# One layer of a hybrid decoder: six of eight pairs of gate projections as seven block products, taken ahead of the branch outputs

## The chip, the cores and the metric

The kernel runs on one core of a Trainium2 chip, as one launch. The metric is the device time of the launch in microseconds (us); lower is better. TensorE is PE in the profile (PEld its weight loads), VectorE DVE, ScalarE ACT, GpSimd POOL; SP issues most transfers.

## The reference, cut to what matters

For 512 prompt rows and 32 sample rows (544 columns once transposed) one layer is computed. The stretch that matters:

```
h = rmsnorm(x, norm1_g) * (1 + sc1) + sh1                  # 544 x 1024
u_in, gate_c, gate_b, q, k, v, g_conv, g_attn = split_projection(h @ w_in)
y_conv = (gate_b * short_conv(gate_c * u_in)) @ w_conv_out  # 1024 -> 1024
y_attn = attn_o @ w_attn_out                                #  512 -> 1024
mixed  = (sigmoid(g_conv) * y_conv + sigmoid(g_attn) * y_attn) @ w_o
x = x + gt1 * mixed          # then a second norm and 16 routed experts
```

## The kernel before

Tokens are columns, split in halves t = 0, 1 of 272 (`HALF`). All projections run as *pieces*, numbered m: one piece makes 128 output channels from 8 chunks (`KC`) of 128 input channels. For accuracy each operand is split into a rounded part and a remainder (`whi`, `wlo`; `hHi`, `hLo`), and `project` multiplies hi with hi, lo with hi and hi with lo: 24 matmuls of 128x128 by 128x272 for a half, 48 for a piece. The result stands in PSUM bank t until some engine has read it (`bank_free[t]`).

Order of the pieces: 0 to 35 q, k, v; 36 to 59 the convolution's inputs; then the branch stage from `C0` = 60 to 91, a loop over f = 0..7 with four pieces each: j = 0 conv output (source `ybHi`/`ybLo`), j = 1 its gate, j = 2 attention output (`oHi`/`oLo`, only 4 chunks, 24 matmuls), j = 3 its gate; then `D0` = 92 to 99 the output projection from `mixHi`/`mixLo`. Half pieces are counted by G = 2m + t. Attention for the prompt and the sample runs between half pieces; its last slots (`decode`, 28 to 31), eight transposes of convolution states and the splitting of `yb` and `oT` stand between piece 59 and the branch stage.

A piece's weights pass through a ring of four (`RING`): SP loads `wraw[m % 4]` once the remainder of piece m - 4 is made; ACT writes `whi` when PE has left that slot (`split_hi`), DVE writes `wlo` (`split_lo`), both for piece m + 3 while PE is at m (`LEAD`). In front of each load of the branch stage's loop SP issues one copy of 1 MB of a key or value cache from DRAM to DRAM (`shift_v3`).

In the branch stage ACT copies every output half out of PSUM (`gyc`) or takes its sigmoid (`gsg`), and DVE multiplies, adds and splits the mix. In the output projection DVE scales each half into `op` (L2218), which is what frees its bank; PE transposes it (`mixed_T`), and `residual` adds it to the rows `x2` of the input. The first `residual` waits for all three loads of `x2` (`xr_in`, 48) and stands in DVE's queue between the two halves of piece 93. SP loads `x2` behind piece 95's weights, after a wait for piece 90 (L825); the modulation rows (`tokt`, `toks`) wait for the last mix (L830); the 32 sample rows come last (L838).

Every engine runs its own queue in the order written; `own` lets DVE wait for its own instruction.

## Time and profile before

| | us |
|---|---|
| time, median of 3 runs (range) | 1102.28 (1101.98 to 1103.21) |
| the profiled execution: span from first to last instruction | 1098.3 |
| outside the span, against the median | 4.0 |
| PE busy in the span | 1069.9 |
| DVE, ACT, POOL busy | 535.5, 355.4, 183.0 |
| branch stage, first matmul to the output projection's first | 572.04 to 740.91 |

The span is that of one profiled execution; the times are of runs without a profile. A view by windows gives the busy time of each engine in a stretch; a timeline lists instructions in order of time, with the idle time ahead of them and what ended it in brackets.

### The profile page before, as it was taken

To read this page: it belongs to the slowest core of one execution; us is meant where nothing else is said; L and a number is where in the kernel's file an instruction comes from. 1 tells how busy PE (TensorE), PEld (TensorE's weight loads), DVE (VectorE), ACT (ScalarE), POOL (GpSimd) and SP (SyncE) were. 2 spreads that over 40 slices of the span, in tenths; PEclk is the share of its full clock that TensorE was granted. 3 is DMA by queue.
4 is the path that set the end of the run, shared out by engine and by line. 5 is a ranking of instruction groups with operands and counts; after the bars stand their busy time and mean duration, and the time that the engine had idled before them with its cause. 6 is when DMAs were issued, how large, how long until landed. Compare 5 with 4: busy or idle time off the path is not lost. (4 is left out here: it accounts for less than half of the span.)

```text
span 1098.3 us, 29565 instructions
## 1 busy us (share of the span) xinstructions
PE 1069.9 (97%) x12413; PEld 929.2 (85%) x12413; DVE 535.5 (49%) x1226; ACT 355.4 (32%) x670; POOL 183.0 (17%) x262
## 2 busy tenths in 40 slices
PE   4899999999999999999999999999999999999997
PEld 3799999999999998898779999999956677777753
DVE  1845565555556545444354444445586333233326
ACT  5623333332433322232244444443332111101112
POOL 1344343343330200000000000000001211121121
PEclk9999999999999999999999999999999999999999
DMA  9969989989888566655999887639679999999996
GB/s 346 341 201 330 387 298 356 387 284 376 310 289 307 175 234 208 235 192 197 410 341 329 281 316 274 205 128 317 240 312 383 368 420 421 421 424 424 422 391 246
DMA packets 161946, 343.95 MB, mean 313 GB/s; under 512 B 11691, under 2 KB 116571, under 8 KB 147310
## 3 DMA queue, kind: packets, MB, share of 16 engines
q1 hardware_dynamic: 149086, 318.64, 78.6%
q0 software_dynamic: 5936, 16.05, 4.1%
q10 hardware_dynamic: 6832, 7.93, 2.1%
q8 instruction: 70, 1.15, 0.4%
q14 instruction: 22, 0.18, 0.0%
HBM read 321.82 MB, written 108.85 MB: 392 GB/s over the span
## 5 line engine op out<-in xcount | busy, mean ns | idle before, releaser
L1035 PE MATMUL psum<-hHi,whi 128*128 128x272 f32 x1200 | 354.1, 295 | 0.3 <-ACT rb L1672 0.3
L1035 PE MATMUL psum<-hLo,whi 128*128 128x272 f32 x1200 | 346.4, 289 | 0.0
L1035 PE MATMUL psum<-hHi,wlo 128*128 128x272 f32 x1200 | 345.9, 288 | 0.0
L1035 PEld LDWEIGHTS psum<-hHi,whi 128*128 128x128 f32 x1200 | 226.2, 189 | 9.1 <-issue 7.5
L1035 PEld LDWEIGHTS psum<-hHi,wlo 128*128 128x128 f32 x1200 | 226.4, 189 | 0.0
L1035 PEld LDWEIGHTS psum<-hLo,whi 128*128 128x128 f32 x1200 | 226.0, 188 | 0.0
L1846 DVE TENSOR_TENSOR wlo<-wraw,whi 128x1024 fp32r<-128x1024 f32 x100 | 133.7, 1338 | 74.9 <-ACT whi L1566 74.8
L1395 PE MATMUL psum<-e,xs 128*32 128x256 f32 x3072 | 169.1, 379 | 0.9 <-DVE xs L2470 0.8
L1395 PEld LDWEIGHTS psum<-e,xs 128*32 128x32 f32 x3072 | 116.3, 110 | 50.6 <-issue 2.5
L2696 POOL DMA_INDIRECT xg<-x_tok,piece x45 | 43.1, 958 | 432.7 <-DMA x_tok<-h 246.9
L1566 ACT ACTIVATE whi<-wraw 128x1024 fp32r<-128x1024 f32 x100 | 104.9, 1051 | 23.7 <-PE psum L1035 23.6
L1408 PE MATMUL psum<-e,hT 128*32 128x256 f32 x1440 | 80.8, 379 | 1.1 <-DMA e<-in_w_dram 0.6
L1775 ACT ACTIVATE sil<-psum 128x128 f32<-128x128 f32 x48 | 13.1, 277 | 198.1 <-PE psum L1395 198.0
L1408 PEld LDWEIGHTS psum<-e,hT 128*32 128x32 f32 x1440 | 55.8, 110 | 23.6 <-DMA e<-in_w_dram 1.7
L2476 DVE TENSOR_TENSOR hid<-sil,psum 128x128 f32<-128x128 f32 x48 | 13.7, 285 | 117.0 <-ACT sil L1775 116.8
L2632 POOL TENSOR_TENSOR t<-rb,ropec 128x272 f32<-128x272 f32 x48 | 38.9, 810 | 165.9 <-ACT rb L1672 145.9
L1672 ACT ACTIVATE rb<-psum 128x272 f32<-128x272 f32 x48 | 18.9, 395 | 104.9 <-PE psum L1035 104.9
L2012 DVE COPY kTs<-psum 128x1024 f32<-128x1024 f32 x18 | 22.1, 1225 | 47.6 <-PE psum L1127 47.6
L2634 POOL TENSOR_TENSOR shb<-shb,ropes 128x272 f32<-128x272 f32 x48 | 40.4, 841 | 1.5 <-DVE shb L2126 1.5
L1035 PE MATMUL psum<-mixHi,whi 128*128 128x272 f32 x128 | 37.5, 293 | 0.0
L1035 PE MATMUL psum<-ybHi,whi 128*128 128x272 f32 x128 | 37.1, 290 | 0.0
L1035 PE MATMUL psum<-mixLo,whi 128*128 128x272 f32 x128 | 37.1, 290 | 0.0
(399 smaller groups left out, 1535.4 us busy)
## 6 DMA issues: line engine op xcount, KB each, us to landing
e<-in_w_dram SPq DMA_DIRECT2D x96, 1024.0 KB, 14.2
wraw<-in_w_in_dram SPq DMA_DIRECT2D x76, 512.0 KB, 6.5
out_dram<-in_cache_k_dram SPq DMA_DIRECT2D x32, 1022.0 KB, 9.7
out_dram<-in_cache_v_dram SPq DMA_DIRECT2D x32, 1022.0 KB, 7.8
adar<-in_w_ada_dram SPq DMA_DIRECT2D x36, 512.0 KB, 7.7
kvr<-in_cache_k_dram SPq DMA_DIRECT2D x8, 2048.0 KB, 7.8
kvr<-in_cache_v_dram SPq DMA_DIRECT2D x8, 2048.0 KB, 11.2
out_dram<-in_cache_k_dram SPq DMA_DIRECT2D x8, 1016.0 KB, 9.7
```

The source lines that it names most:

```text
L1035: mm = pe.matmul(psum[:, t, 0:HALF], w[:, slot, k, :], x[:, k, cols], start=(k == 0 and n == 0), stop=(k == k_n - 1 and n == 2))
L1395: mm = pe.matmul(psum[32 * n:32 * n + 32, g, 0:2 * P].rearrange("p (w f) -> p w f", w=2), xs[:, q, k, 32 * g:32 * g + 32], (e13[q] if w13 ...
L1408: mm = pe.matmul((psum[:, 3 + g, 0:DQ] if u else first_y(g))[32 * n:32 * n + 32], hT[:, fc, 32 * g:32 * g + 32], w2_[:, fc, DQ * n:DQ * n ...
L1566: act.activation(whi[:, slot], wraw[:, slot], ACT.Copy).then_inc(hi_done, 1)
L1672: act.activation(dst, psum[:, t, 0:HALF], ACT.Copy).then_inc(bank_free[t], 1)
L1775: act.activation(sil[:, g, :], psum[:, g, 0:P], ACT.Silu).then_inc(sil_done, 1)
L1846: dve.tensor_tensor(wlo[:, slot], wraw[:, slot], whi[:, slot].bitcast(F32), ALU.subtract)\
L2012: dve.tensor_copy(kTs[:, 8 * P:16 * P], turned[:, 8 * P:16 * P]).then_inc(ktr_dve, 1)
L2476: dve.tensor_tensor(hid[:, g, :], sil[:, g, :], psum[:, g, P:2 * P], ALU.mult).then_inc(hid_done, 1)
L2632: pool.tensor_tensor(t1[:, t, :], rb[:, t, :], ropec[:, cols], ALU.mult).then_inc(rot_done, 1)
L2634: pool.tensor_tensor(shb[:, t, :], shb[:, t, :], ropes[:, cols], ALU.mult)\
L2696: pool.indirect_dma_start(xg[:, q, g, :], None, x_pieces, bass.IndirectOffsetOnAxis(piece[:, q, g:g + 1], 0)).then_inc(xg_in[q], 16)
```

## The change

The gate projections come first: pieces 60 to 75 are the 8 pairs (conv gate, attention gate), then 8 attention outputs (from `O0` = 76), then 8 conv outputs (from `Y0` = 84). Pairs 0 and 1 are ordinary pieces. The other six (`PAIRS`) are made by Strassen's method in Winograd's form: weights of a pair as 2 x 2 blocks (output piece by input half), `h` as 2 x 2 blocks (input half by token half), seven products of 4 chunks each, 12 matmuls for a product (4 chunks by three passes). The four sums of weight blocks are made by POOL for each pair, the four sums of `h` blocks once, three by DVE in `column_sums` and one by POOL. ACT and DVE split every operand (`operand_hi`, `operand_lo`, `columns_hi`, `columns_lo`); products rotate through four PSUM banks and DVE adds them up (`added`), ACT keeping two. Sigmoids are taken in place in SBUF for the six pairs. DVE multiplies the outputs with the gates straight from PSUM. The decode slots 28 to 31 and the state transposes now stand between half pieces 120 to 123. The whole stage is written out instead of looped. The cache copies keep their place, one ahead of each load from piece 64 on. Regions for the gates now lie where `x2` will be, and `x2`'s load waits for the last mix (`g_lo`, 16).

Not shown below: the placement of the buffers, `half_lo` (the remainder of a 4-chunk piece), `columns_hi` and `columns_lo` (split of a column sum), `operand_hi` (ACT's copy, waits for `pool_sum` or the load, and for the product of the pair before that used the slot), the use of one semaphore for several (`logits_pe`, `moved_act`, `rows_pe`).

```diff
+G_P = 2 * KC
+O0 = C0 + G_P
+Y0 = O0 + KC
+PAIR_F0 = 2
+PAIRS = KC - PAIR_F0
+PAIR0 = C0 + 2 * PAIR_F0
+QUART = KC // 2
+ORDER = ("A11", "A12", "S2", "S1", "S3", "S4", "A22")
+AT = {name: i for i, name in enumerate(ORDER)}
+KEPT = {"A11": 1, "S1": 2}
+ADDED = {"A12": 1, "S2": 2, "S3": 4, "S4": 6, "A22": 7}
...
+                if C0 + RING <= m < D0:
+                    shift_v3(m - C0 - RING)
+                last = m - RING
+                if PAIR0 <= last < O0:
+                    n = (last - PAIR0) // 2
+                    sp.wait_ge(w_lo, 7 * n + 7)
+                    sp.wait_ge(pool_sum, 4 * n + 5)
+                else:
+                    sp.wait_ge(lo_done, nth(last) + 1)
+                sp.dma_start(piece_place(m), piece_source(m)).then_inc(raw_in[m % RING], 16)
+                if m < C0 + RING:
+                    cache_units(m)
                 if m == D0 + RING - 1:
 
-                    sp.wait_ge(grp, 2 * (D0 - 1))
+                    sp.wait_ge(g_lo, 2 * KC)
                     for a in (0, 2):
                         sp.dma_start(x2[:, a:a + 2, :], xall_v[:, a:a + 2, :]).then_inc(xr_in, 16)
...
-            pe.wait_ge(yo_lo, KC)
-            with pe.Fori(0, KC) as f:
-                for j in range(RING):
-                    pe.wait_ge(lo_done, 4 * f + (C0 + j + 1))
-                    if j == 2:
-                        pe.wait_ge(yo_lo, KC + 1)
-                    xhi, xlo = ((ybHi, ybLo), (hHi, hLo), (oHi, oLo), (hHi, hLo))[j]
-                    for t in range(2):
-                        project(None, j, xhi, xlo, t, k_n=AC if j == 2 else KC, free=4 * f + (C0 + j))
+            h_halves = [[(hHi[:, QUART * r:QUART * r + QUART, HALF * c:HALF * c + HALF],
+                          hLo[:, QUART * r:QUART * r + QUART, HALF * c:HALF * c + HALF]) for c in range(2)] for r in range(2)]
+            moving = {"A11": h_halves[0][0], "A12": h_halves[1][0], "S2": (hTHi[1], hTLo[1]), "S1": (hTHi[0], hTLo[0]),
+                      "S3": (hTHi[2], hTLo[2]), "S4": h_halves[1][1], "A22": (hTHi[3], hTLo[3])}
...
+            def paired(n):
+
+                for i, name in enumerate(ORDER):
+                    r = 7 * n + i
+                    pe.wait_ge(w_lo, r + 1)
+                    if n == 0 and name in built:
+                        pe.wait_ge(t_lo, built[name])
+                    if r >= 4:
+                        product_read(r - 4)
...
+                    xhi, xlo = moving[name]
+                    for k in range(QUART):
+                        for j, (w, x) in enumerate(((whalf, xhi), (wlow, xhi), (whalf, xlo))):
+                            mm = pe.matmul(psum[:, r % 4, 0:HALF], w[:, i, k, :], x[:, k, :],
+                                           start=(k == 0 and j == 0), stop=(k == QUART - 1 and j == 2))
+                    mm.then_inc(w_pe, 1)
+
+            for n in range(PAIRS):
+                paired(n)
+            for m in range(O0, D0):
+                pe.wait_ge(lo_done, nth(m) + 1)
+                if m == O0:
+                    pe.wait_ge(yo_lo, 1)
+                elif m == Y0:
+                    pe.wait_ge(yo_lo, KC + 1)
+                for t in range(2):
...
+                    if m < Y0:
+                        project(m, m % RING, oHi, oLo, t, k_n=AC, free=nth(m))
+                    else:
+                        project(m, m % RING, ybHi, ybLo, t, free=nth(m))
...
+            def gates_sigmoid(n, part):
+
+                act.wait_ge(p_dve, 7 * n + 6 + part)
+                out = gates[PAIR_F0 + n][:, part, :]
+                act.activation(out, out, ACT.Sigmoid).then_inc(gate_done, 1)
+
...
+            for n in range(PAIRS):
+                if n == 0:
+                    columns_hi(2, 1, pool_sum)
+                operand_hi(n, "S3")
+                operand_hi(n, "S4")
+                kept(n, "A11", p1, 2)
+                operand_hi(n, "A22")
+                if n == 0:
+                    columns_hi(3, 3, t_sum)
+                else:
+                    gates_sigmoid(n - 1, 0)
+                following(n, 0)
+                following(n, 1)
+                kept(n, "S1", p5, 5)
+                if n:
+                    gates_sigmoid(n - 1, 1)
+                if n == 1:
+                    act.wait_ge(so_ev, 4)
+                    act.wait_ge(yb_done, 2 * KC)
+                    act.activation(oHi[:, :, :], oT[:, :, :], ACT.Copy).then_inc(yo_hi, 1)
+                following(n, 2)
+                following(n, 3)
...
+            for m in range(O0, D0 + 1):
+                if m >= O0 + 1:
+                    split_hi_at(m + LEAD)
+                if m < O0 + QUART:
+                    if m == O0:
+                        act.wait_ge(w_pe, 7 * PAIRS)
+                        act.wait_ge(yb_done, 2 * KC)
+                    for k in range(2 * (m - O0), 2 * (m - O0) + 2):
+                        act.activation(ybHi[:, k, :], yb[:, k, :], ACT.Copy).then_inc(yo_hi, 1)
...
+            def operand_lo(n, name):
+
...
+                dve.tensor_tensor(wlow[:, i], src, whalf[:, i].bitcast(F32), ALU.subtract).then_inc(w_lo, 1)
...
+            def column_sums():
+
+                dve.wait_ge(spv_pe, K_UNITS)
+                dve.wait_ge(new_out, 16 * GROUPS * (AC + 1))
...
+                own(dve.tensor_tensor(t1_[:, :, :], b12h, b11h, ALU.subtract))
+                own(dve.tensor_tensor(hTtmp[1][:, :, :], b12l, b11l, ALU.subtract))
+                own(dve.tensor_tensor(t1_[:, :, :], t1_[:, :, :], hTtmp[1][:, :, :], ALU.add))
+                dve.sem_inc(t_sum, 1)
+                own(dve.tensor_tensor(t2_[:, :, :], b22h, t1_[:, :, :], ALU.subtract))
+                own(dve.tensor_tensor(t2_[:, :, :], t2_[:, :, :], b22l, ALU.add))
+                dve.sem_inc(t_sum, 1)
+                dve.wait_ge(so_pe, 2)
+                own(dve.tensor_tensor(t4_[:, :, :], b21h, t2_[:, :, :], ALU.subtract))
+                own(dve.tensor_tensor(t4_[:, :, :], t4_[:, :, :], b21l, ALU.add))
+                dve.sem_inc(t_sum, 1)
...
+                if G == slot_of["O", 1] + DEC_G0:
+                    column_sums()
+                if G == 2 * PAIR0 - 4:
+                    operand_lo(0, "A11")
+                    operand_lo(0, "A12")
+                if G == 2 * PAIR0 - 2:
+                    columns_lo(1, 2)
+                    columns_lo(0, 2)
+
+            def added(n, name, out, other):
+
+                r = 7 * n + AT[name]
+                dve.wait_ge(w_pe, r + 1)
+                dve.wait_ge(p_dve, 7 * n + ADDED[name] - 1)
+                dve.tensor_tensor(out, psum[:, r % 4, 0:HALF], other, ALU.add).then_inc(p_dve, 1)
+
...
+            for n in range(PAIRS):
+                if n:
+                    added(n - 1, "A22", gate_part(n - 1, 1, 0), u3[:, :])
+                operand_lo(n, "S2")
+                operand_lo(n, "S1")
+                if n == 0:
+                    columns_lo(2, 3)
+                operand_lo(n, "S3")
+                dve.wait_ge(p_act, 2 * n + 1)
+                added(n, "A12", gate_part(n, 0, 0), p1[:, :])
+                operand_lo(n, "S4")
+                added(n, "S2", u2[:, :], p1[:, :])
+                operand_lo(n, "A22")
+                if n == 0:
+                    columns_lo(3, 4)
+                dve.wait_ge(p_act, 2 * n + 2)
+                dve.wait_ge(p_dve, 7 * n + 2)
+                dve.tensor_tensor(u25[:, :], u2[:, :], p5[:, :], ALU.add).then_inc(p_dve, 1)
+                if n + 1 < PAIRS:
+                    operand_lo(n + 1, "A11")
+                added(n, "S3", u3[:, :], u2[:, :])
+                dve.wait_ge(p_dve, 7 * n + 4)
+                dve.tensor_tensor(gate_part(n, 1, 1), u3[:, :], p5[:, :], ALU.add).then_inc(p_dve, 1)
+                added(n, "S4", gate_part(n, 0, 1), u25[:, :])
+                if n + 1 < PAIRS:
+                    operand_lo(n + 1, "A12")
+                if n == 1:
+                    dve.wait_ge(yo_hi, 1)
+                    dve.tensor_tensor(oLo[:, :, :], oT[:, :, :], oHi[:, :, :].bitcast(F32), ALU.subtract).then_inc(yo_lo, 1)
...
+            for i in range(LEAD):
+                half_lo(O0 + i)
+            for m in range(O0, D0):
+                if m + LEAD < Y0:
+                    half_lo(m + LEAD)
+                else:
+                    split_lo((m + LEAD) % RING, nth(m + LEAD) + 1)
+                if m < Y0:
+                    f = m - O0
+                    if m == O0:
+                        dve.wait_ge(gate_done, 2 * PAIRS)
                     for t in range(2):
...
+                        part = gates[f][:, 1, HALF * t:HALF * t + HALF]
+                        dve.wait_ge(grp, 2 * nth(m) + t + 1)
+                        dve.tensor_tensor(part, psum[:, t, 0:HALF], part, ALU.mult).then_inc(bank_free[t], 1)
+                    if f < QUART:
+                        for k in range(2 * f, 2 * f + 2):
+                            dve.wait_ge(yo_hi, k + 2)
+                            dve.tensor_tensor(ybLo[:, k, :], yb[:, k, :], ybHi[:, k, :].bitcast(F32),
+                                              ALU.subtract).then_inc(yo_lo, 1)
+                    continue
+                f = m - Y0
+                for t in range(2):
+                    cols = slice(HALF * t, HALF * t + HALF)
+                    if f == 0 and t == 0:
+                        dve.wait_ge(state_out, 16 * (2 * GROUPS + 2))
+                    elif f >= 1:
+                        dve.wait_ge(g_lo, 2 * f - 1 + t)
+                    dve.wait_ge(grp, 2 * nth(m) + t + 1)
+                    dve.tensor_tensor(gmx[:, t, :], psum[:, t, 0:HALF], gates[f][:, 0, cols], ALU.mult)\
+                       .then_inc(bank_free[t], 1)
+                    dve.wait_ge(bank_free[t], nth(m) + 1)
+                    own(dve.tensor_tensor(gmx[:, t, :], gmx[:, t, :], gates[f][:, 1, cols], ALU.add))
+                    hi = mixHi[:, f, cols]
+                    own(dve.tensor_scalar(hi, gmx[:, t, :], 1.0, None, ALU.mult))
+                    dve.tensor_tensor(mixLo[:, f, cols], gmx[:, t, :], hi.bitcast(F32), ALU.subtract).then_inc(g_lo, 1)
...
+            pool.wait_ge(so_pe, 2)
+            pool.wait_ge(spv_pe, K_UNITS)
+            pool.wait_ge(rows_ev, 3)
+            for n, (out, part) in enumerate(((hTsum[2], hHi), (hTtmp[3], hLo))):
+                pool.tensor_tensor(out[:, :, :], part[:, high, cols[1]].bitcast(F32), part[:, low, cols[1]].bitcast(F32),
+                                   ALU.subtract).then_inc(zrow_done, 1)
+            pool.wait_ge(zrow_done, 4 * AC + 4)
+            pool.tensor_tensor(hTsum[2][:, :, :], hTsum[2][:, :, :], hTtmp[3][:, :, :], ALU.add).then_inc(pool_sum, 1)
+
+            for n in range(PAIRS):
+                m = PAIR0 + 2 * n
+                a, b = wraw[:, m % RING], wraw[:, (m + 1) % RING]
+                s1, s2, s3, s4 = (wsum[:, AT[name]] for name in ("S1", "S2", "S3", "S4"))
+                pool.wait_ge(raw_in[(m + 1) % RING], 16 * ((m + 1) // RING + 1))
+                pool.wait_ge(raw_in[m % RING], 16 * (m // RING + 1))
+                if n:
+                    pool.wait_ge(w_pe, 7 * (n - 1) + AT["S1"] + 1)
+                else:
+                    pool.wait_ge(grp, 2 * (PAIR0 - RING + AT["S1"] // 2 + 1))
+                pool.tensor_tensor(s1, b[:, low, :], b[:, high, :], ALU.add).then_inc(pool_sum, 1)
+                pool.wait_ge(pool_sum, 4 * n + 2)
+                pool.tensor_tensor(s2, s1, a[:, low, :], ALU.subtract).then_inc(pool_sum, 1)
+                if n:
+                    pool.wait_ge(w_pe, 7 * (n - 1) + AT["S4"] + 1)
+                else:
+                    pool.wait_ge(grp, 2 * (PAIR0 - RING + AT["S4"] // 2 + 1))
+                pool.wait_ge(pool_sum, 4 * n + 3)
+                pool.tensor_tensor(s4, a[:, high, :], s2, ALU.subtract).then_inc(pool_sum, 1)
+                pool.tensor_tensor(s3, a[:, low, :], b[:, low, :], ALU.subtract).then_inc(pool_sum, 1)
```

## Rows read from the trace of the kernel before

**Rows 1.** The page: busy time by slice, and granted clock.
```profile
PE   4899999999999999999999999999999999999997
PEclk9999999999999999999999999999999999999999
```

**Rows 2.** Waits of PE: total, times, longest, us.
```profile
PE psum L1035 <- ACT rb L1672: 0.3, 1, 0.3
```

**Rows 3.** Windows: the branch stage; columns PE, PEld, DVE, ACT, POOL, PEclk, DMA share, GB/s.
```profile
572.10:740.90 168.80, 168.80 (x1345) 168.80 (x1345) 73.57 (x111) 78.69 (x112) 1.03 (x2) 1.00 0.75 257
```

**Rows 4.** Timeline of PE ahead of the branch stage: start, duration, instruction, idle before.
```profile
571.13 1.08 PE L1187 MATMUL psum<-ident,ps__110 128*128 128x32 f32 x8 [0.27 <-DVE ps__110 L2037]
```

**Rows 5.** Groups by line and shape: busy us, mean ns of one, idle before.
```profile
L1846 DVE TENSOR_TENSOR wlo<-wraw,whi 128x1024 fp32r<-128x1024 f32 x100 | 133.7, 1338 | 74.9 <-ACT whi L1566 74.8
...
L2172 DVE TENSOR_TENSOR gmx<-gsg,gyc 128x272 f32<-128x272 f32 x16 | 7.1, 443 | 14.7 <-ACT gsg L1698 14.7
...
L2049 DVE TENSOR_TENSOR ybLo<-yb,ybHi 128x544 fp32r<-128x544 f32 x8 | 5.3, 720 | 0.8 <-ACT ybHi L1680 0.7
...
L2159 DVE TENSOR_TENSOR oLo<-oT,oHi 128x2176 fp32r<-128x2176 f32 x1 | 2.4, 2425 | 2.1 <-ACT oHi L1688 2.1
...
L1566 ACT ACTIVATE whi<-wraw 128x1024 fp32r<-128x1024 f32 x100 | 104.9, 1051 | 23.7 <-PE psum L1035 23.6
...
L1698 ACT ACT_TABLE_LOAD x8 | 10.3, 1283 | 0.1
...
L2632 POOL TENSOR_TENSOR t<-rb,ropec 128x272 f32<-128x272 f32 x48 | 38.9, 810 | 165.9 <-ACT rb L1672 145.9 <-issue 17.7 <-POOL QB L2647 2.2
...
L2652 POOL COPY kTn<-kT 128x32 f32<-128x32 f32 x12 | 2.5, 206 | 12.7 <-DVE kT L1961 12.6
```

**Rows 6.** Timeline of DVE around 218 us.
```profile
219.94 0.47 DVE L2126 STREAM_SHUFFLE shb<-rb 128x272 f32<-128x272 f32 x1
220.88 1.73 DVE L1846 TENSOR_TENSOR wlo<-wraw,whi 128x1024 fp32r<-128x1024 f32 x1 [0.47 <-ACT whi L1566]
```

**Rows 7.** Timeline of POOL in the same stretch.
```profile
220.03 0.77 POOL L2632 TENSOR_TENSOR t<-rb,ropec 128x272 f32<-128x272 f32 x1 [0.66 <-POOL QB L2647]
220.75 0.77 POOL L2634 TENSOR_TENSOR shb<-shb,ropes 128x272 f32<-128x272 f32 x1
```

**Rows 8.** Windows of DMA: a branch-stage stretch, the output projection's start, the experts.
```profile
651.00:660.00 9.00, 9.00 (x74) 9.00 (x73) 4.96 (x10) 4.45 (x7) 0.00 (x0) 1.00 0.90 320
...
736.00:755.00 19.00, 19.00 (x154) 18.99 (x153) 8.67 (x18) 3.32 (x5) 0.00 (x0) 1.00 0.98 311
...
900.00:950.00 50.00, 50.00 (x932) 36.58 (x928) 17.91 (x49) 6.91 (x18) 8.68 (x10) 1.00 1.02 421
```

**Rows 9.** Timeline of SP's DMA queue at the start of the output projection.
```profile
735.09 0.81 SPq L827 DMA_DIRECT2D x<-in_x_prompt_dram  x2
...
743.50 0.34 SPq L832 DMA_DIRECT2D tokt<-mod_rows  x1
...
745.28 2.70 SPq L838 DMA_DIRECT2D x<-in_x_sample_dram  x1
```

**Rows 10.** Timeline of DVE in the output projection's second piece.
```profile
754.82 0.09 DVE L2189 MEMSET sqp<- 128x40 f32 x1 [4.13 <-DMA x<-in_x_sample_dram]
...
756.13 0.17 DVE L2221 TENSOR_TENSOR op<-psum,modT 128x32 f32<-128x32 f32 x1
```

**Rows 11.** Timeline of PE at the transposes behind it.
```profile
756.56 0.60 PE L1269 MATMUL psum<-ident,op 128*128 128x128 f32 x4
```

**Rows 12.** Timelines of PE: equal matmul groups at the start, and the last matmuls.
```profile
15.96 3.54 PE L958 MATMUL psum<-adarD,cT 128*32 128x128 f32 x64 [1.79 <-DMA adarD<-in_w_ada_dram]
23.04 1.95 PE L958 MATMUL psum<-adar,cT 128*32 128x128 f32 x64
...
1091.38 0.28 PE L1524 MATMUL psum<-stat,fold 128*128 128x1 f32 x2
```

**Rows 13.** Window at the end; columns as in Rows 3.
```profile
1094.00:1095.00 1.00, 0.00 (x0) 0.00 (x0) 0.81 (x1) 0.00 (x0) 0.00 (x0) 0.73 0.95 366
```

More of the change, by code:

```diff
@@ L238, in _build @@
     toks_at -= toks_at % 32
-    assert masks_at <= toks_at and toks_at + YB_EARLY * NT * 4 <= rope_at
     zrow = Region(top - 2048 - 64)("zrow", [P, D // 2])
-    ybHi = Region(toks_at)("ybHi", [P, KC, NT], F32R)
     ybLo = Region(yb_at)("ybLo", [P, KC, NT], F32R)
+    oLo = Region(oT_at)("oLo", [P, AC, NT], F32R)
+    r = Region(yb_at + KC * NT * 4)
+    ybHi = r("ybHi", [P, KC, NT], F32R)
+    r = Region(masks_at)
+    early_gates = [r(f"sg{f}", [P, 2, NT]) for f in range(2)]
+    assert r.at <= rope_at
+    oHi = r("oHi", [P, AC, NT], F32R)
+    assert r.at <= top - 2048 - 64
     r = Region(c_region)
@@ L860, in _ @@
             load_e2(0, 0)
-            for j in range(RING):
-                shift_v3(slice(KC - 1, KC), j)
-            sp.wait_ge(grp, 2 * N_P)
+            for i in range(RING * (KC - 1), RING * KC):
+                shift_v3(i)
+            sp.wait_ge(grp, 2 * nth(N_P))
             sp.dma_start(iota[:, :], k_small[:, 96:96 + TS]).then_inc(late_in, 16)
@@ L1610, in decode @@
                                    accum_out=sst[:, half, 2:3]).then_inc(ss_exp, 1)
-            for G in range(2 * C0):
+            for G in range(2 * PAIR0):
                 m, t = divmod(G, 2)
@@ L1700, in _ @@
-            split_hi_at(D0 + LEAD)
+                if kind(m) == "g":
+                    f, j = divmod(m - C0, 2)
+                    act.wait_ge(grp, G + 1)
+                    act.activation(gates[f][:, j, HALF * t:HALF * t + HALF], psum[:, t, 0:HALF], ACT.Sigmoid)\
+                       .then_inc(bank_free[t], 1)
+                if G == STATES_G:
+                    act.wait_ge(rows_pe, 2)
+                    for n in range(2):
+                        act.activation(ltok[:, 512 * n:512 * n + 512], psum[0:18, 6 + n, :], ACT.Copy).then_inc(rows_ev, 1)
@@ new lines, in kept, with following @@
+            def kept(n, name, dst, free):
+                r = 7 * n + AT[name]
+                act.wait_ge(w_pe, r + 1)
+                if n:
+                    act.wait_ge(p_dve, 7 * (n - 1) + free)
+                act.activation(dst[:, :], psum[:, r % 4, 0:HALF], ACT.Copy).then_inc(p_act, 1)
+            def following(n, i):
+                if n + 1 < PAIRS:
+                    for name in (("A11",), ("A12",), (), ("S2", "S1"))[i]:
+                        operand_hi(n + 1, name)
+                else:
+                    split_hi_at(O0 + i)
@@ L2054, in _, with columns_lo @@
+            def columns_lo(i, at):
+                dve.wait_ge(t_hi, at)
+                dve.tensor_tensor(hTLo[i][:, :, :], hTsum[i][:, :, :], hTHi[i][:, :, :].bitcast(F32), ALU.subtract)\
+                   .then_inc(t_lo, 1)
+            for G in range(2 * PAIR0):
                 decode(G - DEC_G0)
```

342 lines of the change are left out of this document (184 added, 158 removed).

## The prediction

> **What bounds the kernel now.** I read the page's slices first, then the waits, then windows of the stage, then timelines for prices. The slices say that PE is busy from the second slice to the last but one, at a granted clock of nine tenths or more [rows 1]. In the waits, the line that holds PE back for a product's bank (L1035) has lost 0.3 us once in the whole kernel [rows 2]. The window of the branch stage makes it exact: PE is busy 168.80 of 168.80 us, 1.00 of the clock, while DVE, ACT and the DMA engines stand idle for much of it [rows 3]. So matmuls saved here shorten the kernel, as long as PE finds its operands. From the same row one matmul takes 168.80 / 1345 = 0.1255 us, so a product of 12 matmuls takes 1.51 us, a half piece of 24 takes 3.01 us, and a pair as seven products 10.54 us.
>
> **Matmuls removed.** An ordinary pair is 96 matmuls, a Strassen pair 84. Six pairs save 72 x 0.1255 = 9.0 us. The 0.27 us that PE waits in the transposes ahead of the stage [rows 4] may go too, since other matmuls now stand between them: -9.3 us in all. ACT loses nearly all of its table loads in the stage (the group shown is 8 at 1.28 us [rows 5]) and many copies out of PSUM. I price that at nothing: ACT works 78.69 of 168.80 us there and PE waits for it nowhere [rows 3].
>
> **The price of a sum, and what POOL does to DVE.** The added work is POOL's and DVE's, both with two inputs in SBUF. DVE alone makes 1024 elements in 1.22 us undisturbed; 544 take 0.72 and 272 take 0.44 us, and 2176 take 2.43 [rows 5]. By that line 512 elements cost 0.69 and 1088 cost 1.29 us. ACT's 512 cost about 0.61. An addition out of PSUM of 272 elements I take at the 0.44 of `gmx`. POOL's nearest rows are 272 elements in 810 ns and a copy of 32 in 206 ns [rows 5]: 2.35 ns an element, with one input against two. A weight sum (512) is then some 1.33 us and a column sum (1088) 2.65; if the 0.81 had no fixed part, 1.5 and 3.2.
>
> The page of groups hides what the two do to each other. DVE's `wlo` at 220.88 took 1.73 us [rows 6]. POOL's operation of 0.77 us had begun at 220.75 [rows 7], so it overlapped `wlo` for 0.64 us, and `wlo` lost 1.73 - 1.22 = 0.51 us: DVE nearly stood still. The shuffle at 219.94, with one input, ran beside POOL's operation of 220.03 in its usual 0.47 us. I therefore charge each POOL operation of this stage in full against DVE's two-input operations that stand ready, and nothing against DVE's additions out of PSUM.
>
> The Trainium skill has a rule for this, which speaks against the change: "SBUF — State Buffer", section "SBUF: two separate sides", calls the shared port pair an exclusive lock held for the whole instruction, between GpSimd and a VectorE operation with two SBUF inputs; the trace agrees, with 0.51 us lost of 0.64. Its page "GPSIMD Engine Reference", § 3.1, has 4497 ns for 2048 fp32 elements on GpSimd. With the fixed part above, that is an estimate of 1.27 and 2.48 us for the two sums, and the total would come about 1 us lower.
>
> **The first pair.** PE has five half pieces between the last transposes and pair 0, 5 x 3.01 = 15.06 us, and wants S2 (third in the order) two products later, at 18.1. By then the shared port must have passed: DVE's seven operations of `column_sums` (7 x 1.29 = 9.0), the remainders of A11 and A12 (1.4), two column remainders (2.6), that of S2 (0.7), together 13.7 us; and POOL's three operations on columns and its first three weight sums (3 x 2.65 + 3 x 1.33 = 12.0), on which S2 itself depends. That is 25.7 us and some 0.5 for hand-overs, against 18.1: PE waits 8.1 us. Up to A22, whose column sum is last, another 0.9: **+9.0 us**. The bounds are 0 (the queues run side by side) and 11.5 (POOL at the upper price).
>
> **The later pairs.** In 10.54 us DVE has seven remainders (4.8), two SBUF additions (0.9) and five out of PSUM (2.2), 7.9 us; POOL has 5.3 us. Two-input work and POOL's together are 11.0 against 10.54, and DVE's queue is in order, so the additions that free the four banks stand behind a blocked remainder. I put the lateness at 0.9 a pair for pairs 3 to 6, 2.3 for the second (it inherits the first's), and a further 2.1 where DVE makes `oLo` at once (2.43 us [rows 5]) ahead of the next pair's remainders: with the parts overlapping, **+7.4 us**, bounds 0.4 and 13. At the entry to piece 76, its remainder stands behind A22's addition in DVE's queue, 0.44 + 0.69 and a hand-over: **+1.3 us**.
>
> **Attention outputs.** A piece lasts 3.01 us. DVE has 0.69 + 2 x 0.44 + 2 x 0.72 = 3.0 us in each of the first four, exactly PE's pace. The DMA engines must bring some 1.5 MB in each 3.01 us (0.5 MB of weights and the 1 MB cache copy ahead of them), 500 GB/s; the most that the trace shows is 421 at a share of 1.02, and this stage reached 320 at 0.90 [rows 8]. At 421 the load lags 0.6 us a piece. Of five pieces the ring hides about half: **+1.5 us**, bounds 0.5 and 4. In the conv outputs (6.02 us a piece) both fit.
>
> **The output projection.** This is a moved step. Now SP issues `x2` at 735.09, 5.8 us before the projection starts at 740.91, then the modulation rows at 743.50 and the sample rows at 745.28 [rows 9]. DVE's first `residual` waits 4.13 us for those last rows, to 754.82 [rows 10]. PE takes the transposes behind it at 756.56 without a wait, with the operand finished only at 756.30 [rows 10, 11]: its slack is some 0.2 us. After the change `x2` waits for the last mix, which DVE makes about 2.2 us into the projection (multiplication, addition, rounding, remainder behind the last half), 8.0 us later than now. The bytes are the same, and the DMA engines are full from 736 to 755 [rows 8], so everything lands 8.0 later. Behind the waiting `residual` in DVE's queue stands the second half's `op` (L2218), which frees the bank and feeds the transposes: **+7.8 us**. The lower bound: 311 GB/s over 18.8 us is 5.8 MB, which at 421 takes 13.9, so 2.9 us remain.
>
> **The clock.** At the end of the kernel the last matmul stands at 1091.38 [rows 12] and the granted clock of the window from 1094 has dropped to 0.73 [rows 13], a fall some 2.8 us after the work ended. A pause of 7.8 us lets it fall to 1.2 GHz. At the start, 64 equal matmuls took 3.54 us behind a wait and 1.95 at full clock [rows 12]: **+1.6 us**. The same after the first pair's pause I price at nothing, as DVE is still what PE waits for there; without that cover it costs 1.6 as well.
>
> **Sum.** -9.3 + 9.0 + 7.4 + 1.3 + 1.5 + 7.8 + 1.6 = +19.3 us. The profiled span of 1098.3 becomes 1117.6; the 4.0 us between span and median stay: 1121.6, say **1121 us**.
>
> **The rivals.** The bound below which this kernel cannot be told from no change is about 0.2%, 2.2 us.
>
> *POOL does not hold DVE* (the one that can end on the other side). DVE's row has one clear case of it, and a remainder may be long for another reason. Then the first pair's 9.0 and the later pairs' 7.4 shrink to `oLo`'s share, about 1: 1121 - 15.5 = 1106. It becomes faster once `x2` lands at the lower bound too, -4.9 and -1.6: 1099. It decides if PE waits for remainders less than 4 us in the stage. Chance 0.16, in half of it not slower.
>
> *The rows of x cost little.* The queue at 736 to 755 still carries cache copies that will be gone by then; the first `residual` waits only 2.9 us more than now and the clock stays: -4.9 - 1.6, 1114 to 1115. Chance 0.16.
>
> *The lateness is given back.* The experts' DMA engines are full at 421 GB/s while PE is busy 50 of 50 us there [rows 8]; if their weights set the pace later on, weights that run ahead during the pauses make up for them, and only the early terms stay: near 1102. Against it, PE does not wait there now. Chance 0.07.
>
> *Steeper prices.* POOL at 1.5 and 3.2 us, attention outputs at 4 us: +2.5, +4, +2.5: 1130. Chance 0.13.
>
> *The products aren't made as said*, for instance matmuls at another pitch than 0.1255 us because operands are parts of larger tiles: nothing in the rows speaks for it; it would move the 9.0 by its share. I fold it into the range.
>
> The forecast holds the remaining 0.48. Its own range is 1115 to 1127. The range for 8 in 10 leaves out the far ends of the first and the last rival: 1100 to 1129. Faster: half of the first rival and some of the third, 0.11. Same: 0.08. Slower: 0.81.
>
> **What would show it.** In the new profile 504 matmuls should stand on one line of paired products. PE should have waits on ACT or DVE for S2 of the first pair of 7 to 9 us, remainders of 512 elements whose mean is well above 0.69 us with POOL's sums beside them, and 1.3 us for a POOL weight sum. DVE's first wait for the sample rows should be about 12 us, with PEclk below 9 after it. Remainders of 0.69 us beside POOL's sums would make the largest terms wrong; a DVE wait near 4 us would remove the projection's; and a window of the experts with PE idle would show that what was lost could be given back.

## The result, and the profile after

| | before | after |
|---|---|---|
| median, us (range) | 1102.13 (1101.52 to 1103.21, 4 runs) | 1128.66 (1126.67 to 1130.05, 4 runs) |
| span of the profiled execution | 1098.3 | 1124.6 |
| PE busy in the span | 1069.9 | 1070.7 |
| DVE, ACT, POOL busy | 535.5, 355.4, 183.0 | 596.3, 338.3, 230.5 |

The kernel became slower by a ratio of 1.0239 (95% interval 1.0224 to 1.0253). 1121 was forecast, with a range of 1100 to 1129, so the sign was right and the size was 7.7 us short: the median lies 0.3 us inside the upper end of the range, and above the forecast's own range of 1115 to 1127. The profiled execution is the fastest of the four, 2.0 us under their median.

The page's slices, as in [rows 1]:

```profile
PE   4999999999999999999997997997999999999997
PEclk9999999999999999999998999998999999999999
```

PE now has three thin slices, each of 28 us: number 22 (the first pair), 25 (the attention outputs) and 28 (the output projection). The waits of PE name them (engine, out and line, what was waited for, then us in total, times and longest). Before there was one such line on a product's bank, with 0.3 us [rows 2]:

```profile
PE psum L1318 <- DVE wlow L2223: 11.2, 7, 5.8
...
PE psum L1069 <- DVE sg L2416: 6.4, 5, 2.5
PE psum L1344 <- DVEq L2490: 5.5, 1, 5.5
...
PE psum L1069 <- DVE wlo L2208: 1.1, 1, 1.1
PE psum L1069 <- DVE op L2474: 1.1, 1, 1.1
```

L1318 is the paired products, with their remainders as holder; L1069 with `sg` the attention outputs, where a bank waits for DVE's multiplication; L1344 the transposes of the output projection. The timeline of PE puts the waits in order of time (start, duration, instruction, idle before):

```profile
602.84 0.59 PE L1318 MATMUL psum<-hHi,whalf 128*128 128x272 f32 x1 [5.75 <-DVE wlow L2223]
...
618.36 0.39 PE L1318 MATMUL psum<-hHi,whalf 128*128 128x272 f32 x1 [1.35 <-DVE wlow L2223]
629.84 0.39 PE L1318 MATMUL psum<-hHi,whalf 128*128 128x272 f32 x1 [0.64 <-DVE wlow L2223]
633.12 0.39 PE L1318 MATMUL psum<-hTHi,whalf 128*128 128x272 f32 x1 [1.52 <-DVE wlow L2223]
...
676.50 0.40 PE L1069 MATMUL psum<-oHi,whi 128*128 128x272 f32 x1 [1.13 <-DVE wlo L2208]
...
700.73 0.36 PE L1069 MATMUL psum<-oHi,whi 128*128 128x272 f32 x1 [2.46 <-DVE sg L2416]
...
779.82 1.12 PE L1344 MATMUL psum<-ident,op 128*128 128x128 f32 x4 [5.49 <-DVEq L2490]
```

The wait of 0.64 recurs at 643.09, 654.56 and 666.05: once in each later pair, at its second product. A wait costs about 0.3 us more than the bracket says: from the start of one matmul to the next it takes 0.92 to 0.94 us there, against 0.1255, and the step behind it takes 0.1 us more than usual. Measured in that way, from start to start, the terms are:

| term | forecast | measured | how measured |
|---|---|---|---|
| matmuls removed | -9.3 | -9.3 | 504 on L1318; at full clock without a wait still 0.1255 apart |
| first pair | +9.0 | +7.6 | 596.80 to 606.63: 9.83 us for 18 steps of 0.1255 |
| later pairs | +7.4 | +7.0 | six waits, 1.6 in the second pair, 1.8 behind `oLo`, 0.9 for each of the other four |
| entry to piece 76 | +1.3 | +1.4 | one wait |
| attention outputs | +1.5 | **+8.2** | 676.50 to 708.81: 32.3 us for 192 matmuls |
| output projection and clock | +9.4 | +8.9 | its first to its last matmul of `mixHi` with `whi`: 61.6, before 52.7 |
| sum | +19.3 | +23.8 | |

The span grew by 26.3 us. Of the 2.5 us that are missing, 0.5 lie ahead of the branch stage (the same group of 8 transposes starts at 556.32 before and 556.85 after), 1.1 behind the last piece, and 0.9 were not located. One term was wrong; the others held to within 1.4 us.

**POOL and DVE.** Groups by line and shape in the window from 601 to 672:

```profile
L2223 DVE TENSOR_TENSOR wlow<-wraw,whalf 128x512 fp32r<-128x512 f32 x18 | 20.4, 1139 | 0.2 <-ACT whalf L1673 0.2
L2223 DVE TENSOR_TENSOR wlow<-wsum,whalf 128x512 fp32r<-128x512 f32 x24 | 15.4, 677 | 0.0
...
L2969 POOL TENSOR_TENSOR wsum<-wraw 128x512 f32<-128x512 f32 x5 | 7.3, 1467 | 34.3 <-PE psum L1318 34.3
...
L2387 DVE TENSOR_TENSOR u<-u,p 128x272 f32<-128x272 f32 x6 | 7.2, 1198 | 4.8 <-ACT p L1815 4.8
```

The same instruction of the same size takes 677 ns when it reads a weight sum and 1139 in the mean when it reads raw weights. What it reads is not the reason: the 18 are a mixture. In the later pairs the remainder of A22, also read from raw weights but made while POOL is idle, takes 0.68 us, and those of the next pair's A11 and A12, made while POOL makes that pair's sums, 1.78 and 1.24. An SBUF addition of 272 elements takes 1198 ns in the mean instead of 440; DVE's additions out of PSUM keep their 0.43 beside POOL. The timelines of DVE and of POOL show one case, with an undisturbed remainder from raw weights as the last line of DVE:

```profile
611.94 1.53 DVE L2387 TENSOR_TENSOR u<-u,p 128x272 f32<-128x272 f32 x1
613.39 1.78 DVE L2223 TENSOR_TENSOR wlow<-wraw,whalf 128x512 fp32r<-128x512 f32 x1
...
622.04 0.68 DVE L2223 TENSOR_TENSOR wlow<-wraw,whalf 128x512 fp32r<-128x512 f32 x1
```

```profile
611.03 2.14 POOL L2969 TENSOR_TENSOR wsum<-wraw 128x512 f32<-128x512 f32 x1 [10.24 <-PE psum L1318]
613.25 1.38 POOL L2971 TENSOR_TENSOR wsum<-wsum,wraw 128x512 f32<-128x512 f32 x1
```

**The attention outputs.** The wait at 700.73 goes back through DVE's and ACT's queues to a load; ACT's timeline, then DVE's:

```profile
697.92 1.06 ACT L1641 ACTIVATE whi<-wraw 128x1024 fp32r<-128x1024 f32 x1 [4.10 <-DMA wraw<-in_w_conv_out_dram]
```

```profile
699.01 1.23 DVE L2004 TENSOR_TENSOR wlo<-wraw,whi 128x1024 fp32r<-128x1024 f32 x1 [3.54 <-ACT whi L1641]
700.15 0.78 DVE L2416 TENSOR_TENSOR sg<-psum,sg 128x272 f32<-128x272 f32 x2
```

The multiplication that frees PE's bank stands in DVE's queue behind a remainder, the one of piece 84, whose rounded part waited for the weights. Their load had been issued at 684.89, behind a 1 MB copy whose issue took 3.28 us. So the wait is put down to `sg`, but what held it was weights that had not landed.

**The rows of x.** SP's queue, and DVE at the first `residual`; before, SP was there at 735.09 and 745.28 [rows 9], and DVE waited 4.13 us [rows 10]:

```profile
759.23 0.82 SPq L861 DMA_DIRECT2D x<-in_x_prompt_dram  x2
760.09 3.03 SPq L854 DMA_DIRECT2D wraw<-in_w_o_dram  x2
...
768.13 3.08 SPq L872 DMA_DIRECT2D x<-in_x_sample_dram  x1
```

```profile
778.24 0.09 DVE L2445 MEMSET sqp<- 128x40 f32 x1 [7.32 <-DMA x<-in_x_sample_dram]
```

Counted from the start of the projection (757.2), the wait ends at 21.0; before it ended at 13.9. That is 7.1 us later, where 8.0 were forecast. DVE's wait is 7.3 and not 12, because DVE itself comes 3.9 us later to it: the remainder of piece 96 at 769.29 had waited 5.28 us for ACT, and ACT for weights. Their load stands behind that of `x2` in SP's queue, and SP, held there by its wait for the last mix, issued it at 760.09; before the change the two loads behind `x2` were issued at 735.95.

### The profile page after: what moved, and what is told of

Read it like the earlier page. It is cut to its first block and busy times, and to the rows that moved or that the text cites. A ratio compares the mean times of both kernels' runs of the same rounds, so it can differ in the third digit from the quotient of the medians.

```text
span 1124.6 us, 29165 instructions
## 1 busy us (share of the span) xinstructions
PE 1070.7 (95%) x12341; PEld 927.9 (83%) x12341; DVE 596.3 (53%) x1309; ACT 338.3 (30%) x657; POOL 230.5 (20%) x289
## 3 DMA queue, kind: packets, MB, share of 16 engines
q8 instruction: 79, 1.29, 0.4%
## 5 line engine op out<-in xcount | busy, mean ns | idle before, releaser
L1069 PE MATMUL psum<-hHi,whi 128*128 128x272 f32 x1008 | 298.8, 296 | 0.3 <-ACT rb L1782 0.3
L1069 PE MATMUL psum<-hLo,whi 128*128 128x272 f32 x1008 | 290.7, 288 | 0.0
L1069 PE MATMUL psum<-hHi,wlo 128*128 128x272 f32 x1008 | 290.2, 288 | 0.0
L1069 PEld LDWEIGHTS psum<-hHi,whi 128*128 128x128 f32 x1008 | 189.8, 188 | 10.8 <-issue 9.1
L1069 PEld LDWEIGHTS psum<-hHi,wlo 128*128 128x128 f32 x1008 | 190.0, 189 | 0.0
L1069 PEld LDWEIGHTS psum<-hLo,whi 128*128 128x128 f32 x1008 | 189.5, 188 | 0.0
L2004 DVE TENSOR_TENSOR wlo<-wraw,whi 128x1024 fp32r<-128x1024 f32 x80 | 109.2, 1366 | 41.5 <-ACT whi L1641 41.2
L1641 ACT ACTIVATE whi<-wraw 128x1024 fp32r<-128x1024 f32 x80 | 84.0, 1052 | 82.7 <-PE psum L1069 59.2
L1069 PE MATMUL psum<-mixHi,whi 128*128 128x272 f32 x128 | 38.2, 299 | 1.1 <-DVE op L2474 1.1
L1069 PE MATMUL psum<-ybHi,whi 128*128 128x272 f32 x128 | 36.9, 288 | 0.9 <-DVE sg L2416 0.9
```

The lines of the kernel that those rows point to most:

```text
L1069: mm = pe.matmul(psum[:, t, 0:HALF], w[:, slot, k, :], x[:, k, cols], start=(k == 0 and n == 0), stop=(k == k_n - 1 and n == 2))
L1641: act.activation(whi[:, slot], wraw[:, slot], ACT.Copy).then_inc(hi_done, 1)
L2004: dve.tensor_tensor(wlo[:, slot], wraw[:, slot], whi[:, slot].bitcast(F32), ALU.subtract)\
```

## Experiments

The kernel before was timed again beside each group of runs: 1102.10 for the first four, 1102.16 for the next four, 1102.85 for the last two. "Less" is less than the 1128.66 of the changed kernel in the table above.

**1. Rows of x as their place comes free (x_early).** `x2` lies where the gates 2 to 7 lay, so its parts can be loaded after 4, 6 and 7 of the 8 conv outputs.

```diff
-                    sp.wait_ge(g_lo, 2 * KC)
-                    for a in (0, 2):
-                        sp.dma_start(x2[:, a:a + 2, :], xall_v[:, a:a + 2, :]).then_inc(xr_in, 16)
+                    sp.wait_ge(g_lo, KC)
+                    sp.dma_start(x2[:, 0:2, :], xall_v[:, 0:2, :]).then_inc(xr_in, 16)
+                if m == D0 + RING:
+                    sp.wait_ge(g_lo, KC + QUART)
+                    sp.dma_start(x2[:, 2:4, :], xall_v[:, 2:4, :]).then_inc(xr_in, 16)
+                    sp.wait_ge(g_lo, 2 * KC - 2)
+                    sp.dma_start(x2[0:NS, TILES, :], xs_v).then_inc(xr_in, 16)
```

> The rows of x are loaded in three parts, each as soon as the gates that lie there are used up (after 4, 6 and 7 of the 8 conv outputs), instead of all after the last one. Theory (the first residual waits for rows that land 8 us later, and PE loses its clock in the pause): DVE's wait for the sample rows falls from 7.3 us to under 1 us, PE's 5.5 us wait at the transposes (L1344) and the stretch at half clock behind it go, and the time falls by 7 to 9 us, to about 1120. Rival (the wait is for the DMA queues at large, which stand full there whatever the order): the rows still land late, the wait stays above 4 us, and the time falls by less than 3 us.

Measured: 1118.84 us (1116.86 to 1119.06), 9.8 less. DVE's wait for the sample rows and PE's wait at the transposes are no longer among the waits, and the projection takes 52.6 us by the same measure, against 52.7 before the change. SP's queue in the same part:

```profile
736.83 0.58 SPq L859 DMA_DIRECT2D x<-in_x_prompt_dram  x1
...
747.72 0.34 SPq L862 DMA_DIRECT2D x<-in_x_prompt_dram  x1
753.41 0.34 SPq L864 DMA_DIRECT2D x<-in_x_sample_dram  x1
```

The theory holds and the rival falls.

**2. The cache copies moved (copies_moved).** The number of copies and bytes is the same.

```diff
-                if C0 + RING <= m < D0:
-                    shift_v3(m - C0 - RING)
+                if C0 + RING <= m < D0 + RING and not O0 + 3 <= m < Y0 + 3:
+                    for _ in range(2 if m in (C0 + 8, C0 + 10, C0 + 12, C0 + 14) else 1):
+                        shift_v3(next(copies))
```

> No cache copy stands ahead of the loads of pieces 79 to 86; four of those eight stand ahead of pair loads (two for one load) and four ahead of the loads of pieces 92 to 95. Theory (the attention outputs are paced by the transfers, 1.5 MB in 3.01 us): the 8.4 us that the stage lost at the attention outputs fall below 2, and the time falls by 6 to 8 us to about 1121, less what the copies cost at their new places. Rival (DVE's queue paces it, 3.0 us of work for each of the first four pieces): the loss stays above 6 us and the time within 2 us of 1128.7.

Measured: 1119.78 us (1118.81 to 1120.45), 8.9 less. No gap above 0.3 us is left in the attention outputs. DVE's queue has the same work there, so it is not what paced them.

**3. The order without the products (order_alone).** `PAIR_F0` is 8: all gate projections are ordinary pieces, in the new order, and the sums are not made.

```diff
-PAIR_F0 = 2
+PAIR_F0 = KC
```

> The new order of the pieces with all sixteen gate projections as ordinary pieces, no block products, no sums. Theory (the terms add): 9.0 us of matmuls come back, the pairs' lateness of 7.9 + 7.0 + 1.4 goes, the attention outputs' 8.4 and the output projection's 8.9 stay: 1128.7 + 9.0 - 16.3 = 1121. First rival (the order costs nothing, the products cost it all): 1102. Second rival (the attention outputs were late because the pairs had delayed SP's loads): their 8.4 goes too, 1113.

Measured: 1110.65 us (1109.37 to 1111.74). The output projection keeps its loss (61.5 us), so the order, with `x2` laid over the gates, costs those 8.8 us without any product. The attention outputs lose nothing, although every cache copy stands where it stood in the changed kernel. The second rival was nearer (1113). SP's queue shows why; first the changed kernel, then this one, loads of pieces 80 to 83 in both:

```profile
676.47 0.38 SPq L854 DMA_DIRECT2D wraw<-in_w_attn_out_dram  x1
...
677.46 0.58 SPq L854 DMA_DIRECT2D wraw<-in_w_attn_out_dram  x1
...
678.66 0.58 SPq L854 DMA_DIRECT2D wraw<-in_w_attn_out_dram  x1
...
680.38 1.14 SPq L854 DMA_DIRECT2D wraw<-in_w_attn_out_dram  x1
```

```profile
653.67 0.38 SPq L854 DMA_DIRECT2D wraw<-in_w_attn_out_dram  x1
659.72 0.38 SPq L854 DMA_DIRECT2D wraw<-in_w_attn_out_dram  x1
665.75 0.38 SPq L854 DMA_DIRECT2D wraw<-in_w_attn_out_dram  x1
671.79 0.38 SPq L854 DMA_DIRECT2D wraw<-in_w_attn_out_dram  x1
```

In the changed kernel PE starts piece 76 at 676.50, when the loads of 80 to 83, a 1 MB copy ahead of each, are just being issued. Without products PE starts it at 669.92: the loads of 80 to 82 had been issued in the 16 us before that, and that of 83 came 1.9 us after it. The windows of both in this stretch (columns as in [rows 3]), the changed kernel first:

```profile
676.00:682.00 6.00, 3.94 (x29) 3.75 (x30) 3.59 (x7) 2.82 (x5) 0.00 (x0) 1.00 1.11 418
...
694.00:700.00 6.00, 4.22 (x33) 3.82 (x31) 2.33 (x4) 1.06 (x1) 0.00 (x0) 1.00 1.16 410
```

```profile
682.00:688.00 6.00, 6.00 (x49) 5.98 (x48) 4.60 (x8) 1.69 (x2) 0.00 (x0) 1.00 1.25 469
```

The DMA share is above 1 in both. What differs is how far the loads run ahead of PE: to piece 82 here, to piece 79 in the changed kernel.

**4. Weight sums on DVE (sums_on_dve).** The four sums of a pair go from POOL's queue to DVE's, two behind S3's addition and two behind S4's.

```diff
-                pool.tensor_tensor(s1, b[:, low, :], b[:, high, :], ALU.add).then_inc(pool_sum, 1)
+                    dve.tensor_tensor(s1, b[:, low, :], b[:, high, :], ALU.add).then_inc(pool_sum, 1)
...
                 added(n, "S3", u3[:, :], u2[:, :])
+                if n + 1 < PAIRS:
+                    weight_sums(n + 1, 0)
```

> The four sums of weight blocks of each pair are made by DVE instead of POOL. Theory (POOL's operation holds DVE's operations with two SBUF inputs): remainders read from the raw weights fall from a mean of 1139 ns to about 690, a POOL operation of 1.5 us becomes a DVE one of 0.69, a pair goes from 11.5 us to 10.7 to 10.8, the first pair starts some 2 us earlier, and the time falls by 4 to 7 us to about 1123. Rival (the remainders are slow for what they read, a raw weight slot under transfer, not for POOL): they stay near 1140 ns, DVE has 2.8 us more in each pair, a pair takes 12 us or more, and the time rises above 1131.

Measured: 1121.98 us (1121.62 to 1122.51), 6.7 less. Groups of this run in the window from 601 to 672:

```profile
L2223 DVE TENSOR_TENSOR wlow<-wsum,whalf 128x512 fp32r<-128x512 f32 x24 | 15.5, 680 | 0.0
L2223 DVE TENSOR_TENSOR wlow<-wraw,whalf 128x512 fp32r<-128x512 f32 x16 | 10.9, 681 | 0.0
...
L2241 DVE TENSOR_TENSOR wsum<-wraw 128x512 f32<-128x512 f32 x5 | 3.4, 680 | 0.0
L2413 DVE TENSOR_TENSOR u<-u,p 128x272 f32<-128x272 f32 x6 | 2.6, 441 | 5.2 <-ACT p L1815 5.2
```

The remainders read from raw weights are back at 681 ns and the addition at 441. The order of DVE's queue changed too, but not what these instructions read. The column sums show the same: the three that still stand beside POOL's take 3.23 to 3.53 us as before, the four behind them 1.29 instead of 2.12 to 2.26. So it was POOL that held them. DVE does more work, and PE waits less: its waits for remainders fall from 11.2 to 4.3 us. The Trainium skill ("SBUF — State Buffer", section "SBUF: two separate sides") has it that a GpSimd operation and a VectorE operation with two SBUF inputs exclude each other on their shared port pair for the whole instruction; both runs agree, with 1.78 us beside POOL's operations against 0.68 without.

**5. Four pairs instead of six (four_pairs).** `PAIR_F0` is 4, so four ordinary pairs stand ahead.

> Only four of the eight pairs are block products; four ordinary pairs (48 us) stand ahead of them instead of two. Theory (the first pair's 7.9 us were the shared sums finishing late, and any cover hides them; every later pair loses 0.93 us to its own remainders): the wait of 5.8 us and the half clock behind it go, 3.0 us of matmuls come back, two pairs' 0.93 go, the attention outputs stay as late as they were: 1128.7 - 7.9 + 3.0 - 1.9 = 1122. Rival (the first pair waits for something that the pair itself sets off, its own transfers or POOL's sums of its weights): a wait of 3 us or more stays ahead of it, and the time is 1126 or more.

Measured: 1121.16 us (1120.27 to 1122.46), 7.5 less. Ahead of the first pair there is no wait at all and no half clock; the later pairs still wait 1.35, 0.64, 1.51 and 0.64, and the entry 1.13. What the first pair waited for was the shared sums, and cover hides it.

**6. Slots given back early (slots_early).**

```diff
-                    sp.wait_ge(w_lo, 7 * n + 7)
+                    sp.wait_ge(w_lo, 7 * n + (7 if (last - PAIR0) % 2 else 2))
```

> The slot of a pair's first piece is given back to SP once its own two remainders and the pair's sums are made, instead of after all seven remainders. The number and bytes of the transfers and their order stay. Theory (the attention outputs are late because the pairs hold the slots long, so that loads and cache copies come in a burst at their end): the loads of pieces 78, 80 and 82 start up to 7 us earlier, and of the 8.4 us at the attention outputs 2 to 5 go: 1124 to 1127. Rival (1.5 MB in 3.01 us is more than the engines can move, whenever the loads start): the same, within 1.5 us of 1128.7.

Measured: 1127.41 us (1126.48 to 1127.94), 1.3 less, at the edge of what can be told. The load of piece 78 did start at 666.14 instead of 670.43, but that of piece 80 stayed at 676.61: it waits for the remainder of piece 76, which DVE makes behind the last pair. The edit did not release the slots of pieces 80 to 83. Its ratio to before, 1.0227, and that of the changed kernel, 1.0239, have intervals that overlap.

**7. Two remainders inside the last pair (remainders_early).**

```diff
                     operand_lo(n + 1, "A11")
+                else:
+                    half_lo(O0)
...
-            for i in range(LEAD):
-                half_lo(O0 + i)
+            half_lo(O0 + 2)
```

> The remainders of the first two attention outputs stand inside the last pair in DVE's queue, where the other pairs make those of the pair behind them, instead of all three behind the last addition. Theory (SP loads pieces 80 and 81 when those remainders free their slots; the loads of 80 to 82 all started at 676.5 to 678.7, with PE already at piece 76): the wait of 1.1 us ahead of piece 76 goes, those loads start some 4 us earlier, and the attention outputs lose 4 to 6.5 us instead of 8.4: about 1125. Rival (only the amount of bytes counts in that stretch): the 1.4 us of the entry go, the rest stays, 1127.

Measured: 1127.83 us (1126.90 to 1129.32), 0.8 less, not to be told from the changed kernel (ratio to before 1.0225, 1.0209 to 1.0240). The entry's wait is gone, but the loads of 80 to 82 start only 3.6, 2.5 and 1.0 us earlier, counted from the first pair's start. ACT's rounded parts of pieces 76 to 78 take the memory of the last pair's operands, and in the changed kernel ACT could round pieces 77 and 78 only at 670.88 and 673.90, after waits for PE. Four waits of 2.89, 0.53, 0.68 and 2.91 us from start to start remain in the attention outputs, and the last was followed by half clock. They took 34.0 us, not less than the 32.3 of the changed kernel. Both the theory's 1125 and its mechanism as the whole cause fall.

**8 and 9. All repairs together (all_two, all_four).** Edits 1, 2, 4 and 6, and `oLo` in two halves in two pairs; with six and with four pairs.

> All the repairs together, with six pairs as block products: rows of x as gates come free, cache copies moved, weight sums on DVE, slots given back early, and the remainder of the attention output in two halves, in two pairs. If the repairs add: 1128.7 - 9.8 - 8.9 - 6.7 = 1103.3 by the three measured ones, 1.5 to 2.5 less for the halved remainder: 1101 to 1102, no different from the kernel before. If they overlap (DVE, now with the sums, keeps the attention outputs waiting): 1106 or more.

> The same repairs with four pairs as block products. Of the first pair's lateness nothing is left (in the run with sums on DVE it was still 3.4 us of waits and some 2 us at half clock), 3.0 us of matmuls come back: about 2.5 us less than the version with six, 1099, faster than before by 0.2 to 0.3 per cent. Rival (the rest of the lateness stands behind the pairs, not ahead of them): 1104 or more.

Measured: all_two 1104.21 us (1103.21 to 1105.88), ratio to before 1.0018 (1.0009 to 1.0027); all_four 1099.96 us (1099.09 to 1100.52), ratio 0.9977 (0.9968 to 0.9986). The version with six is 2 to 3 us above the sum of the repairs: they overlap in part (what the halved remainder brings was not timed by itself), and four waits of 0.68 to 0.96 us from start to start are left in its pairs beside 2.43, 0.88 and 1.38 in the first. all_four came within 1 us of its forecast. PE's waits of all_four that stand in the stage:

```profile
PE psum L1321 <- DVE wlow L2226: 1.3, 2, 0.7
...
PE psum L1072 <- DVE wlo L2211: 1.1, 1, 1.1
```

**10. all_four with edit 7 (all_four_early).**

> The version with four pairs and all repairs, and these early remainders as well. In its trace the entry to piece 76 is the largest of three waits that are left in the stage (1.43 us from start to start, against 0.125). If the remainder moved is the holder: 1.2 us less, 1098.8. Rival (the remainder inside the last pair delays that pair's own additions, which free the banks): the wait moves there, the same as without.

Measured: 1099.16 us (1098.67 to 1099.63), ratio 0.9966 (0.9954 to 0.9978); the wait at the entry is gone. This is the fastest version: 0.34% below the kernel before.

## Why the prediction was right, and where it was not

The sign and five of the six terms were right for the reasons given. That the time fell inside the range was partly luck: one term was five times its forecast, and 2.5 us lie in no term.

**The bound.** PE was the bound and matmuls saved are time saved: 6.0 us of them remain with four pairs, and all_four_early returns 3.7 of it. Two waits of 0.96 us from start to start are left in its pairs, which are some 1.9 of the 2.3 that are missing.

**What POOL does to DVE.** Right, and shown by experiment 4. It was read from a single pair of rows [rows 6, 7]. The terms that rest on it were 9.0 and 7.4, measured 7.6 and 7.0. The later pairs held in their parts too: 1.6 us for the second (2.3 forecast), 1.8 behind `oLo` (2.1), 0.9 for each other wait (0.9). The price of a POOL sum was put at 1.33 us; its four lines have means of 1.37 to 1.53 in the five later pairs. The two rows that it was read from, 810 ns for 272 elements and 206 for 32, give 2.52 ns an element and not 2.35, and so 1.41 us for a weight sum and 2.86 for a column sum. DVE's 1.22 us for 1024 elements stands in none of the rows shown, whose mean is 1.34; the trace has it, for instance at 606.85 in the kernel before. In the first pair PE already waited at A11, since its remainder stands behind `column_sums` in DVE's queue, and not at S2 as forecast; the shared work, 25.7 us by the forecast, ran from 582.47 to the remainder of S2 at 606.3, 23.9 us. In the timeline of DVE a column sum priced at 1.29 us takes 3.23 and 3.51 beside POOL's:

```profile
582.47 3.23 DVE L2237 TENSOR_TENSOR hTsum<-hHi 128x1088 f32<-128x1088 f32 x1
585.73 3.51 DVE L2238 TENSOR_TENSOR hTtmp<-hLo 128x1088 f32<-128x1088 f32 x1
```
The clock was priced at nothing there, as hidden. It fell, and 17 matmuls stood some 0.23 us apart, 1.7 us more than at full clock, which are in the 7.6. Little of it was hidden: by 24 steps of 0.1255 PE would have wanted S2 at an estimated 605.9, its remainder was ready at 606.35, and PE reached it at 607.68. A window just behind the wait:

```profile
602.80:604.00 1.20, 1.16 (x5) 1.16 (x6) 1.20 (x2) 0.00 (x0) 0.00 (x0) 0.50 0.00 0
```

**The step that failed: attention outputs.** "Of five pieces the ring hides about half" gave 1.5 us, with bounds of 0.5 and 4; it was 8.2. The demand was put too high for half of the stage: a load of an attention output is 256 KB and one of a conv output 512 KB, so with the copy of 1022 KB it is 1.3 MB for pieces 80 to 83 and 1.6 for 84 to 87. That is not what failed. The ring was taken to be as full at piece 76 as in a stage of ordinary pieces, and it was not: a pair keeps both its slots and its operand buffers until near its end, so the loads of 80 to 83 came out together with PE already at piece 76, each behind a 1 MB copy, where order_alone had issued them up to piece 82. Experiments 2 and 3 show that the loss needs both, the copies (without them there: no loss) and the pairs ahead (ordinary pieces ahead, all copies in place: no loss). The 421 GB/s taken as the engines' most was exceeded too: 469 over 6 us in order_alone, at a share of 1.25. Which of the pair's holds delays the loads most was not isolated. Giving back one slot or moving two remainders alone brought 1.3 and 0.8 us.

**The output projection.** Right, in mechanism and size (8.9 of 9.4), and experiment 1 takes all of it away. But its parts were others: 5.8 us from start to start at the transposes instead of a pause of 7.8, 1.4 at a bank that waited for `op` behind the late weights of piece 96, which the prediction did not have, and what is left, some 2.0, for the clock. The 1.6 us for the clock came from a row that does not show it: in the stretch of the 64 matmuls that took 3.54 us [rows 12] the granted clock of the kernel before is 1.00. It came out near the measured cost by luck. This is what the clock did here, columns as in [rows 3]:

```profile
781.00:783.00 2.00, 2.00 (x11) 2.00 (x11) 1.17 (x2) 0.80 (x1) 0.00 (x0) 0.50 0.64 171
```

**The rivals.** "POOL does not hold DVE" fell with experiment 4. "The rows of x cost little" fell with experiment 1. "The lateness is given back" fell: behind the last piece the span is 1.1 us longer, not shorter. "Steeper prices", 1130, came nearest in the number, but not for its reasons: its 1.5 us for a weight sum is near the mean of 1.46, yet the pairs cost less than forecast and not 6.5 us more, and its 4 us for the attention outputs is half of what they lost.

## What to carry to other kernels

A method that saves matmuls spends the slack of the engines behind it: count not only their busy time but when the buffers of a block are all given back, and what the next stage then has in hand. Work with two SBUF inputs should stay on one of DVE and POOL; moving 0.69 us sums onto the busier engine was the faster choice. Where one buffer is laid over another, load it in the parts in which the old one comes free.

## What the runs showed of the hardware

Short pauses can cost the clock. In sums_on_dve PE waited 1.80 us ahead of 630.09 and then ran at 1.2 GHz until 633.7, some 1.6 us lost; all_two lost it after 2.15 us at 599.00, and slots_early after 2.94 at 699.83. In the changed kernel a pause of 2.46 us ahead of 700.73 [the timeline above] left it at 2.4 GHz. In remainders_early a pause of 2.60 ahead of 682.60 left it there too, and one of 2.63 ahead of 701.96 did not. So the length of the pause alone did not decide. In sums_on_dve:

```profile
630.09 0.39 PE L1318 MATMUL psum<-hTHi,whalf 128*128 128x272 f32 x1 [1.80 <-DVE wlow L2223]
```

```profile
631.00:632.00 1.00, 1.00 (x6) 1.00 (x6) 1.00 (x3) 0.00 (x0) 0.00 (x0) 0.50 0.00 0
```

SP's issue of a 1 MB copy took 0.52 us just ahead of the attention outputs of the changed kernel and 2.5 to 4.4 us from 681.57 on, and the small load that stands behind the copy was issued that much later. The DMA share there was 0.87 to 1.16 over 6 us; that full queues are the reason was not shown.
